# Softmax sums folded into the epsilon of the heads' norms, convolution spreads over four PSUM banks, heads' square roots behind the last exp

## The chip, the cores and the metric

The kernel runs on one core of one Trainium2 chip. The metric is device time of that core in microseconds (us), the median over several executions. A profile comes from one more execution; its span runs from the first to the last instruction. Engine names are those of the profile: PE is TensorE (PEld its weight loads), DVE is VectorE, ACT is ScalarE, POOL is GpSimd, SP is SyncE, which issues the weight DMAs.

## The reference, cut to what matters

One residual block over 512 tokens of width 1024, all in float32: a first SwiGLU half step, a mixing layer, a second SwiGLU half step and a final norm. The change touches the end of the mixing layer only:

```python
y_a = short_conv_mixer(xb, xc, xu, conv_w)          # 512 wide, 8 groups of 64
y_b = mla(...)                                      # 4 heads of 128: softmax(q k) v, causal by chunks of 64
y_a = group_rmsnorm(y_a, out_norm_g[:512], 8)
y_b = group_rmsnorm(y_b, out_norm_g[512:], 4)       # one norm per token and head
x = x + gate2 * (concatenate([y_a, y_b]) @ w_out)

def group_rmsnorm(y, g, n):                         # y as (tokens, n, width)
    return y * rsqrt(mean(y * y) + EPS) * g         # EPS = 1e-6
p = softmax(sc)                                     # exp(sc - max) / sum(exp(sc - max))
```

Each head's output goes straight into a norm of its own. With e the unnormalised exponentials, s their sum and o = e v, the head is o/s, and its norm is (o/s) / sqrt(mean(o*o)/s² + EPS) = o / sqrt(mean(o*o) + EPS s²).

## The kernel before, in words

Activations lie transposed (features on the 128 partitions, 512 tokens along the free dimension). Every float32 product is made of three fp32r matmuls: each operand is kept as a high part, rounded to fp32r by ScalarE, and a low part, the rest, subtracted by VectorE or GpSimd; `three` (L759) issues high·high, high·low, low·high. Transposes, column sums and spreads are single float32 matmuls, which the profile records as two rows each.

Nothing is scheduled at run time. Each engine has one list of instructions written out by hand, and semaphores join them, so a wait holds everything behind it on its engine. The lists around the change:

- TensorE: `scores_and_turns(h)` alternates four score products of head h+1 (`scores`, L759, and a mask matmul, L1038; query tiles of 512, 384, 256 and 128 keys) with four groups of transposes of the exponentials of head h (`turn`, L1058). `head_product(h)` multiplies by the values. `conv_spread(j)` (L1018) spreads the inverse group roots of convolution tile j over a PSUM bank. `head_sum(h)` (L778) sums the squares of head h into four columns of bank 7 (`norm_bank`); `norm_spread` (L796) spreads the inverse root over the whole of bank 7. `out_steps(o, ks)` is a part of output product o, with two chains of three matmuls for each k.
- VectorE: `maximum` (L1619, L1622) feeds each exp. `divide(h)` (L1628, L1633) takes the reciprocal of the four sums of head h and scales the four tiles of `probs` in place; the transposes wait for it. `turned_lo` (L1638) makes the low part of the transposed exponentials. `apply_conv(j)` (L1598) multiplies the convolution's tile by its gain and the spread in bank 7, `apply_head(h)` (L1243, low part L1234) does so for a head. `inverse` (L1222) is the reciprocal of the root.
- ScalarE: `exp` (L621, with the row sum as its accumulated output), `turned_hi` (L628), high parts `conv_hi` and `head_norm_hi` (L439), `root` (L429), a Sqrt of the column sums, and the high parts of the weights of the output products (`unit_hi`, L415). Exp and Sqrt need different activation tables; a change of table is an ACT_TABLE_LOAD row.
- GpSimd: low parts of the first convolution tiles and of output weights, in the order conv 0, weights of output product 0, conv 1, conv 2, weights 1, conv 3, weights 2, 3, 4 (L395 and L388).

All four convolution spreads, the four column sums and the four head spreads share bank 7. So `conv_spread(j)` waits for `apply_conv(j-1)`, and `head_sum(0)` waits for `apply_conv(3)`:

```python
pe.wait_ge(u_ready, AP_CONV + j)          # conv_spread(j)
norm_sum(N_HEAD + h, gsq, AP_BASE[N_HEAD] + h)   # head_sum(h): waits u_ready
```

VectorE reaches `apply_conv(3)` after `divide(2)`. The order of TensorE here is: scores and turns 1, product 1, conv_spread(3), head_sum(0), scores and turns 2, norm_spread of head 0, product 2, output product 0, and so on.

Of the kernel before, what the change touches and what calls it, by code (L numbers as in the profile page):

```python
# [22 lines left out]
ALU = mybir.AluOpType  # L23
# [3 lines left out]
P = 128  # L27
# [5 lines left out]
TT = SEQ // P  # L33
# [64 lines left out]
def hybrid_block(nc, x, c, positions, ada_w, ada_b, norm_ffn1_g, ffn1_w1, ffn1_w3, ffn1_w2, norm_mix_g,  # L98
                 w_in, conv_w, q_norm_g, w_uq, kv_norm_g, w_ukv, out_norm_g, w_out, norm_ffn2_g,
                 ffn2_w1, ffn2_w3, ffn2_w2, final_norm_g, consts, out):  # L100
    with ExitStack() as ctx:
# [47 lines left out]
        group_rms = at("group_rms", [P, CT, TT, 2])  # L149
        group_r = at("group_r", [P, CT, TT, 2])  # L150
        nmax_s = at("nmax_s", [P, HEADS * TT])
        nmax = at("nmax", [P, HEADS * TT])
        rsum = at("rsum", [P, HEADS * TT])
        rinv = at("rinv", [P, HEADS * TT])
        u_at = top[0]
# [78 lines left out]
        s_done, max_ready, nmax_ready = sem("s_done"), sem("max_ready"), sem("nmax_ready")  # L234
        exp_ready, rinv_ready, p_ready = sem("exp_ready"), sem("rinv_ready"), sem("p_ready")
        t_done, pth_ready, ptl_ready = sem("t_done"), sem("pth_ready"), sem("ptl_ready")
# [20 lines left out]
        X_BANK = (0, 1, 2, 3, 4, 5, 6, 0)  # L257
        CONV_BANKS = ((0, 1, 2), (3, 4, 6))

        OUT_BANK = (0, 1, 4, 5, 6, 2, 3, 0)  # L260
# [148 lines left out]
        def _(act):  # L409
# [16 lines left out]
            def root(n, width):  # L426

                act.wait_ge(col_done, n + 1)
                act.activation(rms[:, :], norm_bank[:, 0:TT], ACT.Sqrt, scale=1.0 / width,  # L429
                               bias=kst[:, K_COLS:K_COLS + 1]).then_inc(rms_ready, 1)  # L430

            def sqrt_table(spare):
# [182 lines left out]
            def exp(h, q):  # L615

                e, i = TT * h + q, TILE_OF[q]
                act.wait_ge(nmax_ready, e + 1)
                if h >= 2:
                    act.wait_ge(t_done, TT * (h - 2) + q + 1)  # L620
                act.activation(probs[:, h % 2, P_OFF[i]:P_OFF[i + 1]], pb[3 + q % 2][:, 0:P * (i + 1)], ACT.Exp,  # L621
                               scale=SCALE, bias=nmax_s[:, e:e + 1], accum_out=rsum[:, e:e + 1]).then_inc(exp_ready, 1)

# [61 lines left out]
            conv_hi(3)  # L685
            root(N_HEAD, V_HEAD)
            head_square(1)
            exps_and_turned(2)
            head_norm_hi(0)
            head_out(2)  # L690
            for q in range(TT):
                turned_hi(3, q)
            unit_hi(U_O + 2)
            root(N_HEAD + 1, V_HEAD)
            head_square(2)
            unit_hi(U_O + 3)
            head_norm_hi(1)
            head_out(3)
            root(N_HEAD + 2, V_HEAD)
            head_square(3)  # L700
            unit_hi(U_O + 4)
            head_norm_hi(2)
            root(N_HEAD + 3, V_HEAD)
            head_norm_hi(3)
# [48 lines left out]
        def _(pe):  # L753
# [259 lines left out]
            def conv_spread(j):  # L1013

                pe.wait_ge(group_r_ready, j + 2)
                pe.wait_ge(u_ready, AP_CONV + j)
                for t in range(TT):
                    last = pe.matmul(cols(norm_bank, t), cols(group_wide[j], t), ident, start=True, stop=True)  # L1018
                last.then_inc(bc_done, 1)
# [31 lines left out]
            def turn(h, q):  # L1051

                i = TILE_OF[q]
                bank_left(h, q)
                pe.wait_ge(p_ready, TT * h + q + 1)
                for kb in range(i + 1):
                    at_ = P_OFF[i] + P * kb
                    last = pe.transpose(turn_bank(h, q)[:, P * kb:P * (kb + 1)], probs[:, h % 2, at_:at_ + P], ident)  # L1058
                last.then_inc(t_done, 1)
# [19 lines left out]
            def head_sum(h):  # L1079
                pe.wait_ge(gsq_ready, h + 1)  # L1080
                norm_sum(N_HEAD + h, gsq, AP_BASE[N_HEAD] + h)

            def out_begin(o):

                unit(U_O + o)
                if o == 0:
                    pe.wait_ge(pl_ready, 3 * HEADS)
                if o == 1:
                    pe.wait_ge(exp_ready, HEADS * TT)
                if o == 2:  # L1090
# [40 lines left out]
            head_product(1)  # L1131
            conv_spread(3)
            head_sum(0)
            scores_and_turns(2)
            norm_spread(N_HEAD)
            head_product(2)

            out_unit(0)
            head_sum(1)
            turn(3, 0)  # L1140
            turn(3, 1)
            out_begin(1)
            out_steps(1, (0, 1))
            turn(3, 2)
            turn(3, 3)
            out_steps(1, (2, 3)).then_inc(unit_done, 1)
            head_product(3)
            norm_spread(N_HEAD + 1)
            out_begin(2)
            out_steps(2, (0, 1))  # L1150
            head_sum(2)
            out_steps(2, (2, 3)).then_inc(unit_done, 1)
            norm_spread(N_HEAD + 2)

            unit(U_O + 3)
            out_steps(3, (0, 1))
            head_sum(3)
            unit(U_O + 4)
            out_steps(4, (0, 1))
            norm_spread(N_HEAD + 3)  # L1160
            out_steps(3, (2,))
            out_steps(4, (2,))
            out_steps(3, (3,)).then_inc(unit_done, 1)
# [37 lines left out]
        def _(dve):  # L1201
# [391 lines left out]
            def apply_conv(j):  # L1593
# [4 lines left out]
                dve.scalar_tensor_tensor(out=ubuf[:, idx % 3, :], in0=yc[:, j, :], scalar=vcol[:, V_OUTG + j:V_OUTG + j + 1],  # L1598
                                         in1=norm_bank[:, :], op0=ALU.mult, op1=ALU.mult).then_inc(u_ready, 1)

# [22 lines left out]

            def divide(h):

                sums = slice(TT * h, TT * (h + 1))
                dve.wait_ge(exp_ready, TT * (h + 1))
                dve.reciprocal(rinv[:, sums], rsum[:, sums]).then_inc(rinv_ready, 1)  # L1628
                dve.wait_ge(rinv_ready, h + 1)
                for q in range(TT):  # L1630
                    e, i = TT * h + q, TILE_OF[q]
                    pr = probs[:, h % 2, P_OFF[i]:P_OFF[i + 1]]
                    dve.tensor_scalar(pr, pr, rinv[:, e:e + 1], None, ALU.mult).then_inc(p_ready, 1)  # L1633

# [35 lines left out]
            maximum(0, 3)  # L1670
            divide(0)
            maxima_and_turned(0)
            head_parts_lo(2)
            divide(1)
            conv_widen(3)
            head_parts_lo(3, (lambda: None, lambda: maximum(2, 0)))
            maxima_and_turned(1, {0: lambda: apply_conv(0), 2: lambda: apply_conv(1), 3: lambda: apply_conv(2)}, first=1)
            divide(2)
            apply_conv(3)
            inverse(N_HEAD)  # L1680
            maxima_and_turned(2)
            divide(3)
            apply_head(0)
            for q in range(TT):
                turned_lo(3, q)
            inverse(N_HEAD + 1)
            apply_head(1)
            inverse(N_HEAD + 2)
            apply_head(2)
            inverse(N_HEAD + 3)  # L1690
            apply_head(3)
# [85 lines left out]
```

## Time and profile before

| | us |
|---|---|
| median of 3 runs | 1039.33 (1037.5 to 1039.48) |
| the profiled execution's own time | 1040.88 |
| its span | 1039.0 |
| PE busy | 1009.1 (97% of the span) |
| DVE busy | 532.2 (51%) |
| ACT busy | 402.8 (39%) |
| POOL busy | 57.8 (6%) |

Busy time is the union of an engine's instructions. Matmuls overlap in the pipeline, so the time that one takes of the stream is the distance from its start to the next start, which is less than its own duration. "PEclk" is the clock granted to TensorE: 1.00 is 2.4 GHz, 0.50 is 1.2 GHz. A bracket at the end of a timeline row gives the idle time before it and what ended it.

### The profile page before, as it was taken

To read this page: it belongs to the slowest core of one execution; us is meant where nothing else is said; L and a number is where in the kernel's file an instruction comes from. 1 tells how busy PE (TensorE), PEld (TensorE's weight loads), DVE (VectorE), ACT (ScalarE), POOL (GpSimd) and SP (SyncE) were. 2 spreads that over 40 slices of the span, in tenths; PEclk is the share of its full clock that TensorE was granted. 3 is DMA by queue.
4 is the path that set the end of the run, shared out by engine and by line. 5 is a ranking of instruction groups with operands and counts; after the bars stand their busy time and mean duration, and the time that the engine had idled before them with its cause. 6 is when DMAs were issued, how large, how long until landed. Compare 5 with 4: busy or idle time off the path is not lost.

```text
span 1039.0 us, 13372 instructions
## 1 busy us (share of the span) xinstructions
PE 1009.1 (97%) x4587; PEld 826.1 (80%) x4587; DVE 532.2 (51%) x717; ACT 402.8 (39%) x573; POOL 57.8 (6%) x82
## 2 busy tenths in 40 slices
PE   6899999999999999999999899999999999999997
PEld 3478888888888888788887787788888888888886
DVE  2777877768753333634376536643443344433332
ACT  5253443443432222432255543444444344422232
POOL 2110111111000000000000310000000000000000
PEclk9899999999999999999999899999999999999998
DMA  9566876678523333123221111233233332333332
GB/s 334 180 208 205 254 228 211 206 223 262 164 90 112 93 93 96 51 84 98 81 68 40 42 42 62 61 101 101 86 96 101 101 96 86 96 94 97 90 109 81
DMA packets 179000, 127.82 MB, mean 123 GB/s; under 512 B 5424, under 2 KB 166002, under 8 KB 178976
## 3 DMA queue, kind: packets, MB, share of 16 engines
q1 hardware_dynamic: 170544, 97.92, 31.4%
q0 software_dynamic: 8432, 29.58, 8.6%
q8 instruction: 14, 0.23, 0.1%
q14 instruction: 10, 0.08, 0.0%
HBM read 125.39 MB, written 2.10 MB: 123 GB/s over the span
## 4 chain that ended last, share of the span: by engine, by line
PE 93%; DVE 3%; ACT 1%; issue 1%; DMA 1%; POOL 0%; DVEq 0%; ACTq 0%; POOLq 0%
PE pb L759 87%; PE pb L796 1%; PE pb L872 1%; PE pb L1058 1%; PE pb L778 1%; DVE hl L1236 1%; DVE ubuf L1243 1%; DMA vec<-in_conv_w_dram 1%; PE pb L803 0%; DVE acc L1393 0%; PE pb L1038 0%; PE pb L887 0%; PE pb L1010 0%; DVE hl L1424 0%; PE pb L1018 0%
## 5 line engine op out<-in xcount | busy, mean ns | idle before, releaser
L759 PE MATMUL pb<-hh,wh 128*128 128x512 f32 x912 | 358.9, 393 | 6.5 <-DVE hl L1424 2.3
L759 PE MATMUL pb<-hl,wh 128*128 128x512 f32 x912 | 355.7, 390 | 0.0
L759 PE MATMUL pb<-hh,wl 128*128 128x512 f32 x912 | 355.7, 390 | 0.0
L1204 DVE TENSOR_TENSOR wl<-raw,wh 128x1024 fp32r<-128x1024 f32 x156 | 191.1, 1225 | 273.8 <-ACT wh L415 273.8
L415 ACT ACTIVATE wh<-raw 128x1024 fp32r<-128x1024 f32 x163 | 172.6, 1059 | 404.6 <-PE pb L759 404.6
L759 PEld LDWEIGHTS pb<-hh,wh 128*128 128x128 f32 x912 | 171.7, 188 | 48.0 <-DVE hl L1236 4.6
L759 PEld LDWEIGHTS pb<-hh,wl 128*128 128x128 f32 x912 | 171.6, 188 | 36.2
L759 PEld LDWEIGHTS pb<-hl,wh 128*128 128x128 f32 x912 | 171.7, 188 | 34.4
L759 PE MATMUL pb<-gh,wh 128*128 128x512 f32 x352 | 137.0, 389 | 0.0
L759 PE MATMUL pb<-gh,wl 128*128 128x512 f32 x352 | 137.0, 389 | 0.0
L759 PE MATMUL pb<-gl,wh 128*128 128x512 f32 x352 | 136.9, 389 | 0.0
L759 PEld LDWEIGHTS pb<-gh,wl 128*128 128x128 f32 x352 | 66.1, 188 | 13.8
L759 PEld LDWEIGHTS pb<-gh,wh 128*128 128x128 f32 x352 | 66.1, 188 | 13.7
L759 PEld LDWEIGHTS pb<-gl,wh 128*128 128x128 f32 x352 | 66.1, 188 | 13.6
L1270 DVE SCALAR_TENSOR_TENSOR acc<-ada_ring,silu_c,acc 128x1024 f32<-128x1024 f32 x49 | 62.9, 1283 | 1.0
L1312 DVE TENSOR_TENSOR gbuf<-sbuf,pb 128x512 f32<-128x512 f32 x44 | 30.2, 686 | 58.3 <-PE pb L759 58.2
L452 ACT ACT_TABLE_LOAD x44 | 56.5, 1283 | 0.8
L424 ACT ACTIVATE sq<-xres 128x512 f32 (+1 forms) x24 | 15.2, 632 | 85.0 <-DVE xres L1322 84.9
L380 POOL DMA_DIRECT2D ada_ring<-in_ada_w_dram x56 | 29.6, 529 | 200.1 <-DVE acc L1268 105.1
L1322 DVE SCALAR_TENSOR_TENSOR xres<-pb,half_gates,xres 128x512 f32 (+1 forms) x16 | 12.0, 751 | 46.0 <-PE pb L759 46.0
L459 ACT ACTIVATE gh<-gbuf 128x512 f32 x44 | 27.9, 633 | 13.7 <-DVE gbuf L1312 13.7
L1315 DVE TENSOR_TENSOR gl<-gbuf,gh 128x512 f32 (+1 forms) x44 | 30.1, 685 | 0.0
(213 smaller groups left out, 724.0 us busy)
## 6 DMA issues: line engine op xcount, KB each, us to landing
raw<-in_ffn_w_dram SPq DMA_DIRECT2D x104, 512.0 KB, 3.8
ada_ring<-in_ada_w_dram POOLq DMA_DIRECT2D x56, 512.0 KB, 5.3
raw<-in_ffn_w_dram SPq DMA_DIRECT2D x32, 448.0 KB, 3.4
raw<-in_w_in_dram SPq DMA_DIRECT2D x17, 512.0 KB, 3.8
ada_start<-in_ada_w_dram SPq DMA_DIRECT2D x16, 512.0 KB, 9.9
raw<-in_w_out_dram SPq DMA_DIRECT2D x8, 512.0 KB, 3.4
x_nat<-in_x_dram SPq DMA_DIRECT2D x4, 512.0 KB, 5.5
out_dram<-o_nat SPq DMA_DIRECT2D x8, 256.0 KB, 2.9
```

The costliest lines, as they stand in the source:

```text
L380: pool.dma_start(ada_ring[:, k % 4, :], adav[:, k, bass.ds(j * D_MODEL + 2 * D_MODEL, D_MODEL)]) \
L415: act.activation(wh[par][:, :], raw[par][:, :], ACT.Copy).then_inc(hi_ready, 1)
L424: act.activation(sq[:, slot, :], src, ACT.Square).then_inc(sq_ready, 1)
L452: act.activation(vcol[:, V_COLS + 9:V_COLS + 10], kst[:, K_COLS:K_COLS + 1], ACT.Sigmoid)
L459: act.activation(gh[:, bass.ds(i, 1), :], gbuf[:, :].unsqueeze(1), ACT.Copy).then_inc(gh_ready, 1)
L759: last = pe.matmul(o, a, b, start=start and j == 0 and t == 0, stop=stop and j == len(pairs) - 1 and t == 2)
L778: last = pe.matmul(norm_bank[:, t:t + 1], src[:, t * P:(t + 1) * P], one_col, start=True, stop=True)
L1204: dve.tensor_tensor(wl[par][:, :], raw[par][:, :], wh[par][:, :].bitcast(F32), ALU.subtract).then_inc(lo_ready, 1)
L1270: dve.scalar_tensor_tensor(out=acc[:, :], in0=src, scalar=silu_c[:, k:k + 1], in1=acc[:, :], op0=ALU.mult, op1=ALU.add).then_inc(ada_step, 1)
L1312: dve.tensor_tensor(gbuf[:, :], sbuf[:, :], pb[1][:, :], ALU.mult).then_inc(g_ready, 1)
L1315: dve.tensor_tensor(gl[:, bass.ds(i, 1), :], gbuf[:, :].unsqueeze(1), gh[:, bass.ds(i, 1), :].bitcast(F32), ALU.subtract).then_inc(gl_read ...
L1322: dve.scalar_tensor_tensor(out=xd, in0=pb[bank][:, :].unsqueeze(1), scalar=gate, in1=xd, op0=ALU.mult, op1=ALU.add).then_inc(x_upd, 1)
```

## The change

1. `divide` is gone. The exponentials go unscaled into the transposes, which now wait for the exp itself, and the row sums are stored in the natural order of the tiles. A new `head_mean(h)` on VectorE makes EPS·s² (four columns, from SBUF), waits for the column sums and adds mean + EPS·s² (four columns, from bank 7); `head_root(h)` on ScalarE takes the Sqrt of that.
2. `conv_spread(j)` writes banks 7, 0, 1, 2 in place of 7 four times; for j > 0 it waits for the low parts of head 3 in place of `apply_conv(j-1)`. The first output products wait for the `apply_conv`s that read their banks.
3. `head_sum(0)` goes behind `scores_and_turns(2)`, and the heads' sums and spreads move to other places among the output products and the transposes of head 3. The roots of ScalarE and the means and inverses of VectorE follow: none stands ahead of the last exp. The low part of VectorE's list is reordered accordingly.

```diff
 CONV_BANKS = ((0, 1, 2), (3, 4, 6))
+CONV_SPREAD_BANK = (7, 0, 1, 2)
+def head_root(h):
+    act.wait_ge(ms_ready, h + 1)
+    act.activation(rms[:, :], head_ms[:, :], ACT.Sqrt).then_inc(rms_ready, 1)
# exp
-    scale=SCALE, bias=nmax_s[:, e:e + 1], accum_out=rsum[:, e:e + 1]).then_inc(exp_ready, 1)
+    scale=SCALE, bias=nmax_s[:, e:e + 1], accum_out=rsum[:, TT * h + i:TT * h + i + 1]).then_inc(exp_ready, 1)
# ScalarE's list
-root(N_HEAD, V_HEAD)
-head_square(1)
 exps_and_turned(2)
+head_root(0)
+head_square(1)
+head_out(2)
 head_norm_hi(0)
-head_out(2)
-for q in range(TT):
-    turned_hi(3, q)
+turned_hi(3, 0)
+turned_hi(3, 1)
+head_root(1)
 unit_hi(U_O + 2)
-root(N_HEAD + 1, V_HEAD)
 head_square(2)
+turned_hi(3, 2)
+turned_hi(3, 3)
+head_norm_hi(1)
 unit_hi(U_O + 3)
-head_norm_hi(1)
+head_root(2)
 head_out(3)
-root(N_HEAD + 2, V_HEAD)
 head_square(3)
+head_norm_hi(2)
+head_root(3)
 unit_hi(U_O + 4)
-head_norm_hi(2)
-root(N_HEAD + 3, V_HEAD)
 head_norm_hi(3)
# TensorE
 def conv_spread(j):
     pe.wait_ge(group_r_ready, j + 2)
-    pe.wait_ge(u_ready, AP_CONV + j)
+    if j == 0:
+        pe.wait_ge(u_ready, AP_CONV)
+    else:
+        pe.wait_ge(pl_ready, 3 * HEADS)
-        last = pe.matmul(cols(norm_bank, t), ...)
+        last = pe.matmul(cols(pb[CONV_SPREAD_BANK[j]], t), ...)
# turn
-    pe.wait_ge(p_ready, TT * h + q + 1)
+    pe.wait_ge(exp_ready, TT * h + q + 1)
# head_sum
-    norm_sum(N_HEAD + h, gsq, AP_BASE[N_HEAD] + h)
+    norm_sum(N_HEAD + h, gsq, AP_BASE[N_HEAD] + h if h > 0 else AP_CONV + 1)
# out_begin
     if o == 0:
-        pe.wait_ge(pl_ready, 3 * HEADS)
+        pe.wait_ge(u_ready, AP_CONV + 3)
     if o == 1:
+        pe.wait_ge(u_ready, AP_CONV + CT)
         pe.wait_ge(exp_ready, HEADS * TT)
# TensorE's list
 conv_spread(3)
+scores_and_turns(2)
 head_sum(0)
-scores_and_turns(2)
+head_product(2)
+out_begin(0)
+out_steps(0, (0, 1, 2))
 norm_spread(N_HEAD)
-head_product(2)
-out_unit(0)
-head_sum(1)
+out_steps(0, (3,)).then_inc(unit_done, 1)
 turn(3, 0)
 turn(3, 1)
+head_sum(1)
 out_begin(1)
 out_steps(1, (0, 1))
 turn(3, 2)
 turn(3, 3)
+norm_spread(N_HEAD + 1)
 out_steps(1, (2, 3)).then_inc(unit_done, 1)
+head_sum(2)
 head_product(3)
-norm_spread(N_HEAD + 1)
+norm_spread(N_HEAD + 2)
 out_begin(2)
 out_steps(2, (0, 1))
-head_sum(2)
+head_sum(3)
 out_steps(2, (2, 3)).then_inc(unit_done, 1)
-norm_spread(N_HEAD + 2)
+norm_spread(N_HEAD + 3)
 unit(U_O + 3)
-out_steps(3, (0, 1))
-head_sum(3)
+out_steps(3, (0, 1, 2))
 unit(U_O + 4)
-out_steps(4, (0, 1))
-norm_spread(N_HEAD + 3)
-out_steps(3, (2,))
-out_steps(4, (2,))
+out_steps(4, (0, 1, 2))
# VectorE
-def divide(h):
-    sums = slice(TT * h, TT * (h + 1))
-    dve.wait_ge(exp_ready, TT * (h + 1))
-    dve.reciprocal(rinv[:, sums], rsum[:, sums]).then_inc(rinv_ready, 1)
-    dve.wait_ge(rinv_ready, h + 1)
-    for q in range(TT):
-        e, i = TT * h + q, TILE_OF[q]
-        pr = probs[:, h % 2, P_OFF[i]:P_OFF[i + 1]]
-        dve.tensor_scalar(pr, pr, rinv[:, e:e + 1], None, ALU.mult).then_inc(p_ready, 1)
+def head_mean(h):
+    sums = slice(TT * h, TT * (h + 1))
+    dve.wait_ge(exp_ready, TT * (h + 1))
+    dve.scalar_tensor_tensor(out=head_eps[:, sums], in0=rsum[:, sums], scalar=EPS, in1=rsum[:, sums],
+                             op0=ALU.mult, op1=ALU.mult).then_inc(eps_ready, 1)
+    dve.wait_ge(col_done, N_HEAD + h + 1)
+    dve.wait_ge(eps_ready, h + 1)
+    dve.scalar_tensor_tensor(out=head_ms[:, :], in0=norm_bank[:, 0:TT], scalar=1.0 / V_HEAD, in1=head_eps[:, sums],
+                             op0=ALU.mult, op1=ALU.add).then_inc(ms_ready, 1)
# VectorE's list: the four divides are gone
 maxima_and_turned(1, {0: lambda: apply_conv(0), 2: lambda: apply_conv(1), 3: lambda: apply_conv(2)}, first=1)
-divide(2)
 apply_conv(3)
+maxima_and_turned(2)
+head_mean(0)
 inverse(N_HEAD)
-maxima_and_turned(2)
-divide(3)
 apply_head(0)
-for q in range(TT):
-    turned_lo(3, q)
+turned_lo(3, 0)
+turned_lo(3, 1)
+head_mean(1)
 inverse(N_HEAD + 1)
+turned_lo(3, 2)
+turned_lo(3, 3)
 apply_head(1)
+head_mean(2)
 inverse(N_HEAD + 2)
 apply_head(2)
+head_mean(3)
 inverse(N_HEAD + 3)
 apply_head(3)
```

## Rows read from the trace of the kernel before

**Rows 1.** The page, its first line.

```profile
span 1039.0 us, 13372 instructions
```

**Rows 2.** Stretches by window: us, then each engine's busy time, granted clock (PEclk), DMA.

```profile
core 0: us, PE busy (x) PEld busy (x) DVE busy (x) ACT busy (x) POOL busy (x), PEclk, DMA share, GB/s
573.00:584.97 11.97, 11.89 (x80) 10.11 (x78) 9.62 (x22) 7.00 (x18) 6.40 (x5) 1.00 0.14 44
584.97:588.06 3.09, 0.00 (x1) 0.03 (x1) 2.94 (x3) 0.05 (x1) 2.20 (x1) 0.96 0.00 0
588.06:594.80 6.74, 6.74 (x23) 5.58 (x24) 1.04 (x4) 3.28 (x6) 1.27 (x1) 0.51 0.25 79
...
600.40:638.38 37.98, 37.97 (x204) 32.38 (x202) 11.37 (x22) 12.17 (x20) 7.19 (x3) 1.00 0.13 42
```

**Rows 3.** Timeline of PE, conv_spread(3) to head_product(2): start, duration, operation.

```profile
583.87 1.10 PE L1018 MATMUL pb<-kst,turned 128*128 128x128 f32 x8
588.06 1.84 PE L778 MATMUL pb<-kst,gsq 128*128 128x1 f32 x8 [3.09 <-DVE ubuf L1598]
589.76 0.77 PE L759 MATMUL pb<-knh,qnh 128*128 128x512 f32 x1
...
596.89 0.39 PE L759 MATMUL pb<-knh,qnh 128*128 128x256 f32 x1 [0.70 <-ACT probs L621]
...
599.30 0.33 PE L1058 MATMUL pb<-kst,probs 128*128 128x128 f32 x1
...
600.41 0.47 PE L759 MATMUL pb<-pth,vh 128*128 128x512 f32 x1
```

**Rows 4.** Timeline of DVE: the divide of head 0, the end of divide(2), apply_conv(3).

```profile
557.25 1.28 DVE L1633 TENSOR_SCALAR probs<-probs,rinv 128x512 f32<-128x512 f32 x4
...
584.90 2.36 DVE L1633 TENSOR_SCALAR probs<-probs,rinv 128x128 f32<-128x128 f32 x1
...
587.18 0.74 DVE L1598 SCALAR_TENSOR_TENSOR ubuf<-yc,vcol,pb 128x512 f32<-128x512 f32 x1
```

**Rows 5.** Timeline of POOL: weight low parts of output products 0, 1 and 4.

```profile
579.46 2.36 POOL L388 TENSOR_TENSOR wl<-raw,wh 128x1024 fp32r<-128x1024 f32 x1
...
584.79 2.38 POOL L388 TENSOR_TENSOR wl<-raw,wh 128x1024 fp32r<-128x1024 f32 x1
...
626.20 2.40 POOL L388 TENSOR_TENSOR wl<-raw,wh 128x1024 fp32r<-128x1024 f32 x1 [6.55 <-ACT wh L415]
```

**Rows 6.** Timeline of PE, scores_and_turns(0): first score, last transpose, head_product(0).

```profile
557.40 0.39 PE L759 MATMUL pb<-knh,qnh 128*128 128x512 f32 x1
...
563.75 0.33 PE L1058 MATMUL pb<-kst,probs 128*128 128x128 f32 x1
564.87 0.47 PE L759 MATMUL pb<-pth,vh 128*128 128x512 f32 x1 [0.78 <-DVE ptl L1638]
```

**Rows 7.** Timeline of PE: a head sum and a spread with their successors, clock 1.00.

```profile
620.85 0.95 PE L778 MATMUL pb<-kst,gsq 128*128 128x1 f32 x8
621.66 0.49 PE L759 MATMUL pb<-hh,wh 128*128 128x512 f32 x1
...
624.52 1.05 PE L796 MATMUL pb<-kst,rrms 128*128 128x128 f32 x8
625.33 0.48 PE L759 MATMUL pb<-hh,wh 128*128 128x512 f32 x1
```

**Rows 8.** Timeline of ACT: the table loads around root(0) and the first exp of head 3.

```profile
588.65 1.28 ACT L429 ACT_TABLE_LOAD   x1
589.95 0.26 ACT L429 ACTIVATE rms<-pb,kst 128x4 f32<-128x4 f32 x1
...
594.77 1.28 ACT L621 ACT_TABLE_LOAD   x1
```

**Rows 9.** Timeline of DVE: operations that run while POOL is busy.

```profile
579.88 0.74 DVE L1598 SCALAR_TENSOR_TENSOR ubuf<-yc,vcol,pb 128x512 f32<-128x512 f32 x1
...
580.85 0.15 DVE L1622 TENSOR_SCALAR nmax_s<-nmax 128x1 f32<-128x1 f32 x1
...
627.11 2.03 DVE L1234 TENSOR_TENSOR hl<-ubuf,hh 128x512 fp32r<-128x512 f32 x1 [0.70 <-ACT hh L439]
```

More of the change, by code:

```diff
@@ L150, in hybrid_block @@
         group_r = at("group_r", [P, CT, TT, 2])
+        head_ms = at("head_ms", [P, TT])
+        head_pad = at("head_pad", [P, 28])
         nmax_s = at("nmax_s", [P, HEADS * TT])
@@ L153, in hybrid_block @@
         rsum = at("rsum", [P, HEADS * TT])
-        rinv = at("rinv", [P, HEADS * TT])
+        head_eps = at("head_eps", [P, HEADS * TT])
         u_at = top[0]
@@ L234, in hybrid_block @@
         s_done, max_ready, nmax_ready = sem("s_done"), sem("max_ready"), sem("nmax_ready")
-        exp_ready, rinv_ready, p_ready = sem("exp_ready"), sem("rinv_ready"), sem("p_ready")
+        exp_ready, eps_ready, ms_ready = sem("exp_ready"), sem("eps_ready"), sem("ms_ready")
         t_done, pth_ready, ptl_ready = sem("t_done"), sem("pth_ready"), sem("ptl_ready")
@@ L685, in _ @@
             conv_hi(3)
-            root(N_HEAD, V_HEAD)
+            exps_and_turned(2)
+            head_root(0)
             head_square(1)
-            exps_and_turned(2)
+            head_out(2)
             head_norm_hi(0)
-            head_out(2)
-            for q in range(TT):
-                turned_hi(3, q)
+            turned_hi(3, 0)
+            turned_hi(3, 1)
+            head_root(1)
             unit_hi(U_O + 2)
-            root(N_HEAD + 1, V_HEAD)
             head_square(2)
+            turned_hi(3, 2)
+            turned_hi(3, 3)
+            head_norm_hi(1)
             unit_hi(U_O + 3)
-            head_norm_hi(1)
+            head_root(2)
             head_out(3)
-            root(N_HEAD + 2, V_HEAD)
             head_square(3)
+            head_norm_hi(2)
+            head_root(3)
             unit_hi(U_O + 4)
-            head_norm_hi(2)
-            root(N_HEAD + 3, V_HEAD)
             head_norm_hi(3)
@@ L1015, in conv_spread @@
                 pe.wait_ge(group_r_ready, j + 2)
-                pe.wait_ge(u_ready, AP_CONV + j)
+                if j == 0:
+                    pe.wait_ge(u_ready, AP_CONV)
+                else:
+                    pe.wait_ge(pl_ready, 3 * HEADS)
                 for t in range(TT):
-                    last = pe.matmul(cols(norm_bank, t), cols(group_wide[j], t), ident, start=True, stop=True)
+                    last = pe.matmul(cols(pb[CONV_SPREAD_BANK[j]], t), cols(group_wide[j], t), ident, start=True, stop=True)
                 last.then_inc(bc_done, 1)
@@ L1598, in apply_conv @@
                 dve.scalar_tensor_tensor(out=ubuf[:, idx % 3, :], in0=yc[:, j, :], scalar=vcol[:, V_OUTG + j:V_OUTG + j + 1],
-                                         in1=norm_bank[:, :], op0=ALU.mult, op1=ALU.mult).then_inc(u_ready, 1)
+                                         in1=pb[CONV_SPREAD_BANK[j]][:, :], op0=ALU.mult, op1=ALU.mult).then_inc(u_ready, 1)
             def apply_head(h):
@@ L1670, in _ @@
             maximum(0, 3)
-            divide(0)
             maxima_and_turned(0)
             head_parts_lo(2)
-            divide(1)
             conv_widen(3)
```

## The prediction

> **What bounds the kernel now.** I read the page first. Its span is 1039.0 us [rows 1], and TensorE works through nearly all of it, so only what TensorE waits for, or does slowly, can be won. The longest waits of TensorE that the change can reach lie in the mixing layer, and its timeline there shows where. The stretch from the last convolution spread to the product of head 2 is the one that matters [rows 3]. conv_spread(3) starts at 583.87; then TensorE stands still for 3.09 us, until head_sum(0) at 588.06, and the row says for whom: VectorE's apply_conv(3). A second wait of 0.70 us comes at 596.89, for an exp. head_product(2) starts at 600.41. The windows by stage add what the timeline doesn't say: before the gap the granted clock is 1.00 (2.4 GHz), and in the 6.74 us after it the mean is 0.51, the level of 1.2 GHz almost all the way [rows 2]. The engine had been idle for 3.09 us just before the clock fell. After 600.40 there are 38 us with 0.01 us of idle time at clock 1.00: nothing to win there, but something to lose.
>
> Why VectorE is late is in its own timeline. The four scalings of divide(0) took 1.28 us together; in divide(2) the smallest of the four, 128x128, took 2.36 us alone, from 584.90 to 587.26, and apply_conv(3) comes straight behind it at 587.18 [rows 4]. In just that time, from 584.79 to 587.17, GpSimd worked on the low part of a weight [rows 5]. So the divide was held until GpSimd was through, the apply was queued behind it, head_sum(0) needed bank 7 from the apply, and the scores of head 3 were queued behind head_sum(0).
>
> This is what the Trainium skill's page "SBUF — State Buffer", section "Who interferes with whom", describes: VectorE and GpSimd share a pair of ports as an exclusive lock, which a scaling from SBUF to SBUF can need. The trace agrees with the 2.36 us.
>
> **The sum, part by part.** I rebuild the stretch from 583.87 to the start of head_product(2), with everything on TensorE in the new order, at clock 1.00.
>
> - conv_spread(3), start to next start: as any spread, 625.33 − 624.52 = 0.81 [rows 7]. Its bank is now 2, its wait is long past (the low parts of head 3 came before the second score of this head), and nothing behind it waits for apply_conv(3).
> - scores_and_turns(2): the same work for head 0's round took 563.75 − 557.40 = 6.35 to the start of the last transpose, with no wait inside [rows 6]. In round 2 it took 599.30 − 589.76 = 9.54 [rows 3]. The excess of 3.19 is the slow clock and the 0.70 wait.
> - From the last transpose to the head product: 564.87 − 563.75 = 1.12 in round 0, where nothing filled the wait for the low part, and 600.41 − 599.30 = 1.11 in round 2, where a spread did [rows 3, 6]. Now head_sum(0) stands there, 621.66 − 620.85 = 0.81 at the full clock, and fits in [rows 7]: 1.12.
>
> Together 0.81 + 6.35 + 1.12 = 8.28, where 600.41 − 583.87 = 16.54 was taken. The spread of head 0, which was hidden in the 1.11, now stands among the steps of output product 0 and costs 0.81. The gain is 16.54 − 8.28 − 0.81 = 7.45 us. Of it 3.09 is the gap, 0.70 the wait for the exp, and 3.66 what the slow clock cost, the refilled pipeline and the late spread set against each other.
>
> The wait for the exp goes for a reason of its own. root(0) stood between the exps of heads 2 and 3, so ScalarE loaded a table at 588.65 and again at 594.77, each 1.28 us, and the second one delayed the exp for which TensorE waited at 596.89 [rows 3, 8]. Behind the last exp one load is left for head_root(0), and nobody waits for it.
>
> The rest costs nothing on the path, with its cover named. The removed divides of heads 0, 1 and 3 held no matmul: TensorE waited for none of them, so they win nothing. The transposes' earlier release wins nothing either, as scores stand ahead of each. conv_spread(1) and (2) may start up to a tenth earlier. The new four-column operations of head_mean are not in the trace. Their nearest rows are the root, 0.26 on 128x4, and a 128x512 scalar_tensor_tensor, 0.74 [rows 8, 9]; I take 0.26, as the overhead is what both kinds share at this size. Head 0's chain from the sum to the inverse is then two VectorE operations, a table load, a root and a reciprocal: 0.52 + 1.28 + 0.52 = 2.3 and some tenths of signalling. Its cover is head_product(2) and three steps of output product 0. Two steps take 624.52 − 621.66 = 2.86 [rows 7], so three take 4.3; the head product has 3840 columns against the 6144 of two steps, an estimated 1.8; 6.1 in all. With 0.74 each the chain grows to 3.3 and is still covered. Heads 1 and 3 have two output steps, 2.86, over a chain of 1.0 (2.0 at the dear end). Head 2 is the tightest: only head_product(3), 1.8, over a chain of 1.0, so 0.8 to spare, or a stall of 0.2 at the dear end. Sums and spreads are neither more nor fewer than before, and the reordered steps of products 3 and 4 are the same matmuls. The last low part that GpSimd makes (output product 4, 2.40 [rows 5]) is asked for when product 2 ends, and used after a spread, 0.81, and three steps, 4.3; with a high part on ScalarE ahead of it, of about 1, it needs 3.4 and has 5.1. SP's loads wait for those low parts alone, so none comes later.
>
> A rule of the skill speaks against the change at one point, and I weigh it. First the rows: with divide(2) gone, VectorE scales the first maximum of head 3 at about 587, while GpSimd is still in the low part of 584.79; such a scaling from SBUF to SBUF, 128x1, took 0.15 at 580.85, inside GpSimd's 579.46 to 581.82, and apply_conv(1) took 0.74 at 579.88 in the same time [rows 5, 9]. Neither was held, so I add nothing. The page and section named above would have that scaling blocked like the divide, as both are tensor_scalar; GpSimd goes on to the convolution's low part, so the exp would come about 1.3 us late and the third score would stall for about 0.7, which makes the sum 6.75 in place of 7.45. The trace speaks against it for this shape.
>
> The sum is made against the profiled execution, whose own time is 1040.88 with a span of 1039.0; the median of the runs is 1039.33, a little below it. I take the gain off the median: 1039.33 − 7.45 = 1031.88, rounded to 1031.9. I take 0.2%, some 2.1 us, as what a measurement of this kernel can tell from no change.
>
> **The rivals.**
>
> *Held behind GpSimd elsewhere.* The new list puts more of VectorE's work beside GpSimd's low parts. Two SBUF operands are enough to be held: the low part of a head took 2.03 at 627.11 while GpSimd worked from 626.20 to 628.60 [rows 5, 9]. The first operation of head_mean reads SBUF twice and stands on the way to a spread. One such hold costs up to 2.4, less the cover of 0.8 to 3.8, so 0 to 1.6 on the path; one or two give 1032.6 to 1034.5, middle 1033.4. For it: the shape. Against it: GpSimd's remaining three low parts start when an output product ends or head 2's rounds are over, mostly beside the low parts of heads, which are needed late.
>
> *The clock falls anyway.* If the spread, transposes and one-column sums of this stretch don't hold 1.00, only the gap and the exp wait are won: 3.79, so 1035.5. Against it: the same mixture ran at 1.00 from 573.00 to 584.97 [rows 2]. The same time results if the usual execution of the kernel before has the gap without the fall.
>
> *No difference.* The bank's wait moves rather than goes: a spread waits for its root. For head 0 the chain would have to be 13 us where I count 2.3. Time 1039.
>
> *Slower.* Place: the transposes of head 3. ScalarE has head_norm_hi(0) ahead of turned_hi(3, 0), so all that follows hangs on norm_spread of head 0, and turn(3, 2) needs the bank that turned_lo(3, 0) frees. A stall of g us there brings the clock down again and costs g + 3.66. It is slower than before by 2.1 once g exceeds 7.45 + 2.1 − 3.66 = 5.9; at g = 7 the time is 1042.5. For it there is only the length of the chain; against it, norm_spread(0) is ready 3.8 us early by the sum above.
>
> **How the numbers follow.** The forecast, 7.45 with tenths around it, has 0.72, with a range of its own of 1031.0 to 1032.8. Held behind GpSimd 0.14; the clock falls anyway 0.08; no difference 0.03; slower 0.03. The predicted time is 1031.9. The bottom of the range is the forecast less the distance of the fastest run from the median, 1031.9 − 1.8 = 1030.1, taken as 1030.3. The top is the clock rival, 1035.5. Left out are the last two cases and the tails. Faster by over 0.2% are the first three: 0.94.
>
> **What would show it.** Right: no idle row ahead of L778; scores of head 3 within 0.9 us of the last convolution spread; granted clock 1.00 from 573 to the end of the output products; round 2 of scores and transposes at 6.35 us; two ACT_TABLE_LOAD rows fewer in this layer; no TensorE wait for L1222. Wrong: a clock of 0.50 anywhere after 585, a VectorE row of over 1 us beside a GpSimd row with TensorE idle behind it, or an idle row ahead of L796.

## The result, and the profile after

The changed kernel takes 1033.02 us (median of 5, 1030.78 to 1033.75) against 1039.33 (median of 5, 1037.5 to 1041.09): the ratio is 0.9935, 95% interval 0.9917 to 0.9952, or 6.8 us less, between 5.0 and 8.6. The forecast was 1031.9, 7.45 us less, with a range of 1030.3 to 1035.5. Both kernels measured once more gave 0.9932 (0.9917 to 0.9947).

The page of the kernel after; its own time was 1033.02:

```profile
span 1031.4 us, 13364 instructions
```

The same stretch of TensorE's timeline as in [rows 3], then the later part with the sums and spreads of heads 0 and 2:

```profile
583.31 1.11 PE L1031 MATMUL pb<-kst,turned 128*128 128x128 f32 x8
584.17 0.47 PE L769 MATMUL pb<-knh,qnh 128*128 128x512 f32 x1
...
590.63 0.33 PE L1071 MATMUL pb<-kst,probs 128*128 128x128 f32 x1
590.80 0.95 PE L788 MATMUL pb<-kst,gsq 128*128 128x1 f32 x8
591.74 0.47 PE L769 MATMUL pb<-pth,vh 128*128 128x512 f32 x1
...
597.83 1.05 PE L806 MATMUL pb<-kst,rrms 128*128 128x128 f32 x8
...
608.53 0.94 PE L788 MATMUL pb<-kst,gsq 128*128 128x1 f32 x8
...
611.31 1.11 PE L806 MATMUL pb<-kst,rrms 128*128 128x128 f32 x8
...
631.83 0.50 PE L769 MATMUL pb<-hh,wh 128*128 128x512 f32 x1 [1.18 <-DVE wl L1218]
```

No row of TensorE from 583.31 up to the last one shown ends in a bracket, so it never stood still there, where [rows 3] had waits of 3.09 and 0.70. The sum of head 0 (590.80) lies between the last transpose and the head product. The windows of the kernel after answer to those of [rows 2]:

```profile
584.97:588.00 3.03, 3.03 (x17) 2.23 (x16) 1.77 (x5) 1.90 (x4) 2.58 (x2) 1.00 0.13 23
588.00:594.00 6.00, 6.00 (x42) 5.38 (x43) 3.31 (x12) 4.78 (x13) 0.00 (x0) 1.00 0.23 79
```

TensorE is busy all the time, at 2.4 GHz, where it had stood still and then run at 1.2 GHz.

VectorE's timeline after, with apply_conv(3), the scaling of head 3's first maximum, the two operations of head_mean(0), the inverse of head 0, and the low part of head 3:

```profile
584.45 0.75 DVE L1612 SCALAR_TENSOR_TENSOR ubuf<-yc,vcol,pb 128x512 f32<-128x512 f32 x1 [2.58 <-PE pb L1031]
...
586.82 0.15 DVE L1636 TENSOR_SCALAR nmax_s<-nmax 128x1 f32<-128x1 f32 x1
...
591.51 0.15 DVE L1642 SCALAR_TENSOR_TENSOR head_eps<-rsum 128x4 f32<-128x4 f32 x1
591.78 0.16 DVE L1646 SCALAR_TENSOR_TENSOR head_ms<-pb,head_eps 128x4 f32<-128x4 f32 x1
593.26 0.18 DVE L1236 RECIPROCAL rrms<-rms 128x4 f32<-128x4 f32 x1 [1.31 <-ACT rms L438]
...
621.28 1.74 DVE L1248 TENSOR_TENSOR hl<-ubuf,hh 128x512 fp32r<-128x512 f32 x1 [0.70 <-ACT hh L447]
```

And GpSimd's, for the rows that run beside the second and the last of these:

```profile
586.25 1.30 POOL L398 TENSOR_TENSOR hl<-ubuf,hh 128x512 fp32r<-128x512 f32 x1
...
620.07 2.41 POOL L391 TENSOR_TENSOR wl<-raw,wh 128x1024 fp32r<-128x1024 f32 x1 [7.77 <-ACT wh L418]
```

The apply waits for its spread (2.58 us of idle VectorE) and no longer sits behind a divide. The scaling took 0.15 inside GpSimd's 586.25 to 587.55. The low part, 0.69 when nothing holds it, took 1.74 beside GpSimd's 620.07 to 622.48; it was ready at 623.02, and the matmul that reads it started at 627.99.

To compare kernels free of what differs elsewhere, I use one distance of their traces below, from the start of the last convolution spread to the first matmul of output product 5, behind its wait of 1.18 us. It is 639.55 − 583.87 = 55.68 before and 631.83 − 583.31 = 48.52 after: 7.16 less, of a span that is 7.6 shorter. "Stretch" is this distance from here on. The second trace of the kernel after had 632.21 − 583.68 = 48.53.

### The profile page after: what moved, and what is told of

The parts are those of the page before. It is cut to its first block, busy times and chain, and to the rows that moved or that the text cites. A ratio compares the mean times of both kernels' runs of the same rounds, so it can differ in the third digit from the quotient of the medians.

```text
span 1031.4 us, 13364 instructions
## 1 busy us (share of the span) xinstructions
PE 1006.6 (98%) x4587; PEld 824.1 (80%) x4587; DVE 523.9 (51%) x705; ACT 400.4 (39%) x571; POOL 57.8 (6%) x82
## 4 chain that ended last, share of the span: by engine, by line
PE 95%; DVE 2%; ACT 1%; issue 1%; DMA 1%; POOL 0%; DVEq 0%; ACTq 0%; POOLq 0%
PE pb L769 88%; PE pb L882 1%; PE pb L806 1%; PE pb L1071 1%; DVE hl L1250 1%; DVE ubuf L1257 1%; DMA vec<-in_conv_w_dram 1%; PE pb L813 0%; PE pb L788 0%; PE pb L1051 0%; PE pb L897 0%; PE pb L892 0%; PE pb L1020 0%; ACT wh L418 0%; PE pb L1031 0%
```

## The experiments

Each was compared with the kernel before on the same chip.

### GpSimd's list alone

```diff
 conv_lo(2)
-unit_lo(U_O + 1)
 conv_lo(3)
+unit_lo(U_O + 1)
 unit_lo(U_O + 2)
```

> The kernel before, with one pair of GpSimd's list exchanged: the low part of convolution tile 3 ahead of the weight low part of output product 1, so that GpSimd waits, idle, for apply_conv(3) while divide(2) runs. Theory A (VectorE's last scaling of divide(2) was held for 2.36 us by GpSimd's weight low part, and all that follows from that): divide(2) takes about 1.3 us as divide(0) did, apply_conv(3) no longer queues behind it and starts when its spread is done, about 585.1; TensorE idles about 1 us ahead of the sum of head 0 in place of 3.09, the clock stays at 1.00, the 0.70 us wait for the exp of head 3 and the table loads stay. Gain about 2.1 + 3.4 = 5 to 6 us, so 1033.5 to 1034.5, most of what the whole change brought. Theory B (the divide is long of itself, or bank 7's chain of waits alone makes the gap): no change, 1039.

Measured: 1036.72, ratio 0.9957 (0.9944 to 0.9971). VectorE's timeline of the kernel before has the whole divide of head 2 in one row:

```profile
582.80 4.46 DVE L1633 TENSOR_SCALAR probs<-probs,rinv 128x512 f32<-128x512 f32 x4
```

Here it has this divide and the apply:

```profile
582.61 2.37 DVE L1633 TENSOR_SCALAR probs<-probs,rinv 128x512 f32<-128x512 f32 x4
584.91 0.73 DVE L1598 SCALAR_TENSOR_TENSOR ubuf<-yc,vcol,pb 128x512 f32<-128x512 f32 x1
```

GpSimd's has the low part of convolution tile 2:

```profile
583.23 1.41 POOL L395 TENSOR_TENSOR hl<-ubuf,hh 128x512 fp32r<-128x512 f32 x1 [0.35 <-ACT hh L439]
```

TensorE's has the sum of head 0:

```profile
585.79 1.02 PE L778 MATMUL pb<-kst,gsq 128*128 128x1 f32 x8 [1.00 <-DVE ubuf L1598]
```

And two windows of it:

```profile
584.00:587.00 3.00, 2.00 (x18) 1.79 (x17) 1.64 (x3) 1.83 (x4) 1.20 (x2) 1.00 0.16 56
587.00:590.00 3.00, 3.00 (x12) 2.04 (x10) 0.90 (x3) 1.45 (x3) 3.00 (x2) 0.60 0.00 0
```

Without an edit to the divide, all four scalings take 2.37 where the kernel before has 4.46 for the four, and the gap is 1.00 where it had been 3.09. So it was GpSimd's weight low part that held the divide's end, as theory A has it. It had expected 1.3 for the four, though: 1.1 us above the undisturbed 1.28 are left, and the low part of convolution tile 2, from 583.23 to 584.64, lies beside them; that it is the cause is read from the times, no run took it away. The gain is 4.5 us by the ratio and not 5 to 6, and the windows show one reason: after a gap of only 1.00 us the clock fell all the same. The stretch is 635.69 − 583.68 = 52.01.

### Part 2 alone: four banks

The edits of the change to `conv_spread`, `apply_conv`, the wait of head_sum(0) and `out_begin`, and no others; the lines that decide:

```diff
+CONV_SPREAD_BANK = (7, 0, 1, 2)
-last = pe.matmul(cols(norm_bank, t), cols(group_wide[j], t), ...)
+last = pe.matmul(cols(pb[CONV_SPREAD_BANK[j]], t), cols(group_wide[j], t), ...)
-norm_sum(N_HEAD + h, gsq, AP_BASE[N_HEAD] + h)
+norm_sum(N_HEAD + h, gsq, AP_BASE[N_HEAD] + h if h > 0 else AP_CONV + 1)
```

> Part 2 of the change alone on the kernel before: the spreads of the convolution go to banks 7, 0, 1, 2 and the sum of head 0 no longer waits for apply_conv(3). Divides and order stay. Theory A (the wait for bank 7 is only one of several that stand behind the held divide): the 3.09 us ahead of the sum are gone, but ScalarE's root of head 0 stays ahead of the exps, behind the high part of apply_conv(3) at about 588.6, so that the first exp of head 3 comes after two table loads at about 592.5; the third score then waits some 4 us for it, the clock may fall again. Gain 0 to 3 us, 1036.5 to 1039.5. Theory B (the bank alone made the gap): the gap doesn't come back, gain 6 us or more, 1033.

Measured: 1039.85, ratio 0.9999 (0.9987 to 1.001): no gain. TensorE's timeline, the third score of head 3, and the window behind it:

```profile
594.00 0.39 PE L760 MATMUL pb<-knh,qnh 128*128 128x256 f32 x1 [3.53 <-ACT probs L622]
```

```profile
596.00:600.00 4.00, 4.00 (x17) 3.67 (x18) 2.57 (x10) 1.38 (x6) 0.00 (x0) 0.50 0.00 0
```

The gap ahead of the sum is gone and stands, 3.53 us long, ahead of the third score: it waits for an exp that ScalarE, by its timeline, makes only after the late apply's high part, the root and two table loads. The clock falls behind it. Theory A holds; the stretch is 55.13.

### Part 1 alone: no divides

The divides and their semaphore are gone, `head_mean` and `head_root` are those of the change, and all lists keep the old order, as here on VectorE:

```diff
-divide(2)
 apply_conv(3)
+head_mean(0)
 inverse(N_HEAD)
 maxima_and_turned(2)
```

> Part 1 of the change alone on the kernel before: no divides, the softmax sums in the epsilon, with sums, spreads and roots where they were and the spreads of the convolution in bank 7. Theory A: apply_conv(3) starts at about 585.1 and the sum of head 0 at about 586, so 1.0 us of idle time in place of 3.09, clock 1.00; the root of head 0 stays ahead of the exps and its two table loads cost up to 0.7 us. Gain 5.5 to 6.2 us, 1033.2 to 1033.8. Theory B (the order of the roots is what pays): gain under 2 us.

Measured: 1035.21, ratio 0.9956 (0.9942 to 0.9969): 4.6 us, less than forecast. TensorE's timeline, with the waits for the apply and for the exp:

```profile
583.77 1.02 PE L785 MATMUL pb<-kst,gsq 128*128 128x1 f32 x8 [0.93 <-DVE ubuf L1605]
...
589.88 0.38 PE L766 MATMUL pb<-knh,qnh 128*128 128x256 f32 x1 [1.00 <-ACT probs L628]
```

And the window with the second wait:

```profile
587.00:590.00 3.00, 2.00 (x12) 1.44 (x12) 1.78 (x5) 2.83 (x5) 0.00 (x0) 1.00 0.28 99
```

The clock stayed at 1.00 in this execution, and the stretch is 632.54 − 581.73 = 50.81. The old order keeps two waits of about 1 us each. VectorE's timeline shows the hold in its other form:

```profile
583.54 1.36 DVE L1635 SCALAR_TENSOR_TENSOR head_eps<-rsum 128x4 f32<-128x4 f32 x1
```

Four columns, 0.15 elsewhere, took 1.36 while GpSimd had a weight's low part:

```profile
582.54 2.34 POOL L390 TENSOR_TENSOR wl<-raw,wh 128x1024 fp32r<-128x1024 f32 x1
```

The operation ended at 584.90, a tenth behind the end of the sum at 584.79. It cost nothing all the same, since ScalarE's root behind it had its table only at 585.65.

### Part 3 alone: the order

The lists of TensorE, ScalarE and VectorE are those of the change, with `root(N_HEAD + h)` for `head_root(h)`, no `head_mean`, and the divides put back. The diff is against VectorE's list of the kernel after:

```diff
+divide(2)
 apply_conv(3)
 maxima_and_turned(2)
-head_mean(0)
+divide(3)
 inverse(N_HEAD)
```

> Part 3 of the change alone on the kernel before: the divides stay (each of them one place ahead of the heads' inverse of its round) and the convolution's spreads stay in bank 7, but sums, spreads and roots stand where the change has them, so nothing but the held apply_conv(3) is late. Theory A: divide(2) is still held by GpSimd until 587.2; TensorE goes on with the scores of head 3, but the maximum of head 3 stands behind divide and apply on VectorE, so its exp ends at about 590 and the third score, due at 588.6, waits about 1.5 us; the clock holds. Gain 5 to 6.5 us, 1033 to 1034.5. Theory B (the divide itself must go): a gap of 3 us again and a fall of the clock, 1038 to 1039.

Measured: 1034.08, ratio 0.9939 (0.9925 to 0.9952): 6.3 us. VectorE's timeline has the divide of head 2, TensorE's the third score of head 3:

```profile
582.55 4.51 DVE L1635 TENSOR_SCALAR probs<-probs,rinv 128x512 f32<-128x512 f32 x4
```

```profile
589.65 0.39 PE L761 MATMUL pb<-knh,qnh 128*128 128x256 f32 x1 [0.91 <-ACT probs L621]
```

The divide is there and is held as long as ever, 4.51 us; yet of its lateness only 0.91 reaches TensorE, and the clock stays at 1.00:

```profile
584.00:600.00 16.00, 15.09 (x89) 12.59 (x88) 9.61 (x21) 7.58 (x19) 4.24 (x3) 1.00 0.14 46
```

The stretch is 633.33 − 583.61 = 49.72, 5.96 of the change's 7.16. Theory A, with a wait shorter than the 1.5 forecast. The run moves the lists of three engines together, so it does not say how much of this is the later sum and how much the later root.

### The gap filled

```diff
 conv_spread(3)
+pe.wait_ge(pl_ready, 3 * HEADS)
+warm(15, 0)
 head_sum(0)
```

> The kernel before, with 15 dummy matmuls of 128x384 in the gap between the last convolution spread and the sum of head 0 (into bank 0, free by then): TensorE waits for the same event, but isn't idle. The output is the same. Theory A (3.66 us of the gain of the change were the price of the slow clock after the gap): the sum of head 0 starts at the same time as before or 0.1 later, the clock stays at 1.00, round 2 of scores and transposes takes 6.4 to 7.1 us in place of 9.54. Gain 3 to 3.7 us, 1035.6 to 1036.3. Theory B (the clock falls by the kind of work in this stretch, not by the idle time): no gain, 1039.

Measured: 1037.63, ratio 0.997 (0.9959 to 0.9982): 3.1 us. TensorE's timeline:

```profile
587.72 1.02 PE L778 MATMUL pb<-kst,gsq 128*128 128x1 f32 x8 [0.53 <-DVE ubuf L1600]
...
593.84 0.39 PE L759 MATMUL pb<-knh,qnh 128*128 128x256 f32 x1 [1.00 <-ACT probs L621]
```

The sum starts no earlier after its spread than before (4.25 us, against 4.19), but the clock is at 1.00 now:

```profile
584.00:600.00 16.00, 14.47 (x90) 12.41 (x89) 10.39 (x22) 8.70 (x19) 4.11 (x3) 1.00 0.11 38
```

Round 2 took 596.25 − 588.61 = 7.64 us to its last transpose, in place of 9.54, where 6.4 to 7.1 was expected. The stretch is 636.51 − 583.47 = 53.04, so 2.64 less: theory A, with less than the 3.66. The wait for the exp is 1.00 in place of 0.70: with faster matmuls ahead of it, TensorE waits longer for the same exp. So part of what the slow clock took had been hidden there.

### The change without the four banks

```diff
-CONV_SPREAD_BANK = (7, 0, 1, 2)
+CONV_SPREAD_BANK = (7, 7, 7, 7)
-if j == 0:
-    pe.wait_ge(u_ready, AP_CONV)
-else:
-    pe.wait_ge(pl_ready, 3 * HEADS)
+pe.wait_ge(u_ready, AP_CONV + j)
-norm_sum(N_HEAD + h, gsq, AP_BASE[N_HEAD] + h if h > 0 else AP_CONV + 1)
+norm_sum(N_HEAD + h, gsq, AP_BASE[N_HEAD] + h)
```

> The changed kernel with part 2 taken back: all four convolution spreads in bank 7, each waiting for the apply ahead of it. Theory A (with the divides gone and the sum of head 0 behind round 2, nothing waits for that bank): same as the changed kernel within 0.3 us, about 1032.5 to 1033. Theory B (four banks carry the gain): the gap ahead of the scores of head 3 comes back in part, 1 to 3 us slower than the changed kernel.

Measured: 1033.35, ratio 0.9932 (0.9919 to 0.9946), the same as the changed kernel beside it (1033.34, 0.9932). The stretch is 630.58 − 582.04 = 48.54 against 48.52. Theory A: the banks bring nothing, alone or with the rest.

The changed kernel itself, measured beside it:

> The changed kernel once more, on the chip of the other runs of this set, as their yardstick: 1032 to 1033.5 by either theory; its trace as on record.

Measured: 1033.34, ratio 0.9932 (0.9917 to 0.9947).

### When a short wait brings the clock down

GpSimd's exchange had shown a fall after 1.00 us, part 1 alone none after 0.93. Both were traced again, unchanged, in single executions:

> The exchange in GpSimd's list once more, for one look. In its first trace a wait of 1.00 us ahead of the sum of head 0 was followed by a fall of the clock to 0.50 for some 3 us, which theory A had not expected. Theory A2 (with a wait this short the fall is a matter of the execution, not of the kernel): another execution can show round 2 at clock 1.00, and then the stretch from the last convolution spread to output product 5 is some 1.7 us shorter than the 52.0 us of the first. Theory B2 (this order of work always brings it down): the fall is there again, 52.0.

> The same kernel a third time, with the same expectations: A2, one of the two repeats at least without the fall; B2, the fall in both.

> Part 1 of the change alone once more, for one look. Its first trace had a wait of 0.93 us at the same place and no fall of the clock; the stretch from the last convolution spread to output product 5 took 50.8 us. Theory A2 (chance of the execution): it may show a fall now, with 52 to 53 us. Theory B2 (the exchange in GpSimd's list alone brings the fall, this kernel never): 50.8 again at clock 1.00.

Windows of the first and the second repeat of the exchange, and of the repeat of part 1:

```profile
587.00:590.00 3.00, 3.00 (x11) 2.13 (x10) 1.02 (x3) 1.17 (x4) 2.43 (x2) 0.50 0.01 3
```

```profile
584.00:587.00 3.00, 3.00 (x13) 2.07 (x13) 0.18 (x1) 2.29 (x4) 2.70 (x2) 0.68 0.00 0
587.00:590.00 3.00, 3.00 (x14) 2.56 (x15) 1.69 (x4) 1.52 (x2) 0.90 (x1) 0.75 0.30 77
```

```profile
587.00:590.00 3.00, 3.00 (x11) 2.23 (x10) 1.02 (x3) 1.19 (x3) 0.43 (x1) 0.50 0.50 175
```

The clock fell in all three, after waits of 1.01, 1.01 and 0.93. With the first traces that is four falls in five executions with a wait of about 1 us at this place. For part 1 the same kernel shows both: so it is a matter of the execution, and its price can be read off one pair of traces, as the stretch was 50.81 without the fall and 634.91 − 583.05 = 51.86 with it, 1.05 us. A2 holds for part 1, a little under its 52 to 53; for the exchange B2 can't be excluded, as it fell three times of three, with stretches of 52.01, 52.01 and 52.33. The falls explain only a part of why both gained less than forecast. Part 1 without a fall is 55.68 − 50.81 = 4.87 below the kernel before, where 5.5 to 6.2 was expected, and the exchange would be at 4.7 with 1.05 given back, where 5 to 6 was. In part 1 the wait for the exp is seen to take a share of the rest, 1.00 in place of 0.70.

### Two attempts to go further

The wait of 1.18 us ahead of product 5 is in both kernels. The first attempt issues product 3 whole:

```diff
-unit(U_O + 3)
-out_steps(3, (0, 1, 2))
-unit(U_O + 4)
-out_steps(4, (0, 1, 2))
-out_steps(3, (3,)).then_inc(unit_done, 1)
-out_steps(4, (3,)).then_inc(unit_done, 1)
+out_unit(3)
+out_unit(4)
```

> The changed kernel with output product 3 issued whole and then product 4, in place of holding back the last step of both. Both kernels wait 1.18 us ahead of product 5 for its weight's parts, which ScalarE may only make once product 3 is through. Theory A: product 3 ends about 4 us earlier, the wait of 1.18 us is gone, and the last step of product 3 just finds the low part of head 3 (ready at 623.0, wanted at 623.6): 1.2 us faster than the changed kernel. Theory B (the low part of head 3, which GpSimd holds up for 1 us, comes too late for the earlier step): a wait of up to 1 us ahead of that step takes the place of the one removed, no gain.

Measured: 1031.42, ratio 0.992 (0.9906 to 0.9934), 1.9 us below the median of the changed kernel beside it. The two intervals, 0.9906 to 0.9934 and 0.9917 to 0.9947, overlap, so the difference rests on the trace. ScalarE's timeline has product 5's high part:

```profile
623.56 1.06 ACT L418 ACTIVATE wh<-raw 128x1024 fp32r<-128x1024 f32 x1 [4.06 <-PE pb L769]
```

Counted from the start of the last convolution spread it starts 623.56 − 581.56 = 42.00 us in, where the kernel after has 629.38 − 583.31 = 46.07, and TensorE has no idle row from that spread up to 645. The held low part of head 3 was ready at 621.28 and its step began at 621.94. From the last convolution spread to the sum of squares of the next norm it is 647.55 − 581.56 = 65.99 us, against 650.77 − 583.31 = 67.46 for the kernel after: 1.47 less.

The second moves one spread on top of that:

```diff
 scores_and_turns(0)
+conv_spread(0)
 head_product(0)
 head_unit(3)
-scores_and_turns(1, {0: lambda: conv_spread(0), 2: lambda: conv_spread(1), 3: lambda: conv_spread(2)})
+scores_and_turns(1, {2: lambda: conv_spread(1), 3: lambda: conv_spread(2)})
```

> The changed kernel with output product 3 issued whole (as in the run before) and the first convolution spread moved from round 1 of scores and transposes to the place ahead of the product of head 0, where TensorE waits 0.78 us for the low part of the last transposed tile. The spread's inputs were ready long before. Theory A: the wait is filled and round 1 is 0.81 shorter: 0.8 us faster than the kernel with product 3 issued whole alone, 2 us faster than the changed kernel, ratio to before about 0.991. Theory B (the move only shifts the wait: with the spread gone, round 1 waits for the exp of head 2 ahead of its third score): no gain over the kernel with product 3 whole.

Measured: 1031.11, ratio 0.9926 (0.9912 to 0.9939), no better than the first attempt. TensorE's timeline:

```profile
561.68 1.06 PE L1031 MATMUL pb<-kst,sq 128*128 128x128 f32 x8
...
576.89 0.33 PE L769 MATMUL pb<-knh,qnh 128*128 128x128 f32 x1 [0.45 <-ACT probs L629]
...
579.67 0.47 PE L769 MATMUL pb<-pth,vh 128*128 128x512 f32 x1 [0.48 <-DVE ptl L1649]
```

The 0.78 ahead of the product of head 0 is filled, but round 1 now waits 0.45 for an exp (ahead of its fourth score, not the third) and 0.48 ahead of its product, where it was 0.31. These two take back 0.62 of the 0.81 that was moved, and in the end nothing is left of it: from the last transpose of round 0 to the product of head 1 it is 579.67 − 561.52 = 18.15 us, against 579.62 − 561.46 = 18.16 in the first attempt. Theory B.

## Why the prediction was right

**Direction, place and mechanism.** TensorE's 3.09 us were lost to a divide held behind GpSimd. GpSimd's exchange shows it directly: 4.46 became 2.37 with the divide untouched, and the gap fell by the same 2.1. Filling the gap shows that the slow clock hung on it. That the 0.70 for the exp was lost to a table load is read from the rows; no run tested it alone. Of the signs named ahead, the scores of head 3 came 0.86 behind the last convolution spread, the clock was 1.00 throughout, and two ACT_TABLE_LOAD rows are gone (one for the exp, one for the root, where there were two each).

**The sum.** The measured 1033.02 lies inside the range but just outside the forecast's own 1031.0 to 1032.8, where the rival "held behind GpSimd" was priced. The trace shows the forecast's mechanism and not the rival's. The rebuilt stretch to the head product was 8.28; it took 591.74 − 583.31 = 8.43, with 0.86 for the spread, 6.46 for the round (6.35 taken) and 1.11. The moved spread of head 0 cost 40.09 − 39.14 = 0.95 from the head product to product 5, where 0.81 was taken. 16.54 − 8.43 − 0.95 = 7.16, against 7.45 forecast: the round was 0.11 longer than taken, the moved spread 0.14 and the convolution's spread 0.05.

**The hidden chains.** The small operations were priced at 0.26 and took 0.15 to 0.20. Head 0's inverse was ready at 593.44, 4.4 us ahead of its spread at 597.83. The tightest, head 2, had its inverse at 610.16 and its spread at 611.31: 1.15 to spare for 0.8 forecast. No spread waited.

**The rule against the change.** The scaling of one column took 0.15 again, this time beside GpSimd's low part of a convolution tile, as the weight's had ended at 586.30; so the row was the right guide. The Trainium skill's page "SBUF — State Buffer", section "Who interferes with whom", says that a tensor_scalar can need the shared ports, when its operands meet certain conditions; for one column the trace shows no hold, at either place. The same section of the Trainium skill says that a VectorE instruction with two SBUF inputs contends with a GpSimd instruction that reads SBUF; the trace agrees, with the 1.36 of part 1 alone and the 1.74.

**The rivals.** Held behind GpSimd elsewhere: it happened, to the low part of head 3 (1.74), off the path, so it cost nothing. The clock falls anyway: not in the changed kernel; but my reason against it was too comfortable, since a wait of 1 us at this place, not only one of 3, was followed by a fall in four of five executions. The forecast needed the gap to go whole, and it did. No difference, slower: no spread waited for its root, so neither came about.

**What the prediction did not separate.** It summed the three parts as one rebuilt stretch. The parts alone gave ratios of 0.9956 (no divides), 0.9999 (banks) and 0.9939 (order), against 0.9932 to 0.9935 for all three. Their gains are not a sum: each of the first two leaves or makes another wait, and behind it the clock. The order alone takes 5.96 of the 7.16 us in the traces, since it puts TensorE's other work between the late apply and whoever needs it. The divides add 1.2 in the traces (by the ratios, 0.9939 and 0.9932 to 0.9935, that is within the noise), the banks nothing.

**Against the medians.** By medians the gain is 6.3, by the ratio 6.8, by spans 7.6. The profiled execution of the kernel before was 1.55 above its median (1040.88 against 1039.33), that of the kernel after was its median, and this covers the 1.3 between the two. Of the 1.1 that the median gain falls short of the 7.45, 0.3 is the sum above; the rest depends on which executions are compared. TensorE also reached the product of head 0 at 564.87 before and at 564.31 after: 0.56 of the 7.6 lies ahead of the changed part. In the other traces with a wait there it was anywhere from 562.53 to 565.46. The window from 15 to 45 us, which the change doesn't touch, first of the kernel before and then of the one after:

```profile
15.00:45.00 30.00, 26.15 (x102) 14.02 (x101) 20.42 (x33) 11.81 (x22) 4.09 (x2) 0.89 0.81 274
```

```profile
15.00:45.00 30.00, 27.41 (x105) 14.29 (x105) 22.24 (x34) 11.78 (x22) 5.17 (x2) 0.83 0.80 271
```

The granted clock there differs in a part that the change leaves alone, but it is the kernel after that has less of it, so this does not explain its 0.56. What sets these differences at the start, and with them the 3 us between the executions of one kernel, was not tested and stays open.

## What to carry to other kernels

A long wait of TensorE, where it bounds the kernel, can be paid twice, as here: once as idle time and once as slow clock after it. Removing only part of the wait can leave the second payment in place. Before an operation is removed because it is late, look at what held it and at which work could stand between it and its reader: reordering hid a 4.5 us divide down to 0.9. And measure the parts together as well as alone, since a wait that is taken away at one place may stand again at the next one.

## What the runs showed that I had not expected

- At the same place of the same kernel, a TensorE wait of 0.93 us was followed by clock 1.00 in one execution and 0.50 in another. No other wait of up to 1.2 us in this layer was followed by a fall: not the 0.78 ahead of the product of head 0, not the 0.91 to 1.00 ahead of the third score of head 3 (parts 1 and 3 alone, the filled gap), and not the 1.18 ahead of output product 5, in any trace that has them. What makes this one place differ was not tested.
- A scalar_tensor_tensor on four columns with both inputs in SBUF took 1.36 us beside GpSimd, nine times its 0.15.
- One fall cost 1.05 us net, though some 3 us ran at half speed, since a later wait shrank from 1.00 to 0.52 us in the same execution.
